# Matmuls of two K-steps interleaved, and weight blocks 160 columns apart in the rotating places

## The reference

```python
m, ... = mixer_even(hn, ...)   # z = h @ w_in (1024 x 2048) ... @ w_out (1024 x 1024)
m, cc  = mixer_odd(hn, ...)    # h @ w_in (1024 x 3072) ... @ w_out (1024 x 1024)
x = x + rmsnorm(m, p['norm_mix_post'][l])
hn = rmsnorm(x, p['norm_ffn_pre'][l])
f = jnp.square(jax.nn.relu(hn @ p['mlp_up'][l])) @ p['mlp_down'][l]
x = x + rmsnorm(f, p['norm_ffn_post'][l])
```

## Time and profile before

| what | value |
|---|---|
| median of 3 runs | 2115.71 us (2115.54 to 2116.01) |
| the profiled execution: its own time | 2116.21 us |
| its span, first to last instruction | 2114.1 us |
| PE busy in the span | 2105.2 us |
| granted TensorE clock, mean | 0.999 |
| DVE, ACT, POOL busy | 1187.2, 718.6, 279.3 us |

### The profile page before, as it was taken

How to read it: one execution, slowest core, us unless ns; L and a number is a source line. 1 busy time by engine, 2 the same in 40 slices (tenths; PEclk the granted TensorE clock), 3 DMA queues, 4 the chain that set the end, 5 groups by cost and what they waited for, 6 DMA issues and landing times.

```text
span 2114.1 us, 33629 instructions
## 1 busy us (share of the span) xinstructions
PE 2105.2 (100%) x13976; PEld 2094.1 (99%) x13976; DVE 1187.2 (56%) x1798; ACT 718.6 (34%) x1225; POOL 279.3 (13%) x307
## 2 busy tenths in 40 slices
PE   9999999999999999999999999999999999999998
PEld 9999999999999999999999999999999999999998
DVE  8766367364755747334953333384566475564336
ACT  6673345132232322333511112352313233232332
POOL 2000000031221312000033232000113022130000
PEclk9999999999999999999999999999999999999999
DMA  4111422111111111141311114131111111111142
GB/s 165 39 38 40 137 78 85 51 51 42 51 48 51 51 51 51 42 141 40 123 51 40 51 50 133 41 122 51 45 52 45 51 51 51 51 51 46 46 142 82
DMA packets 209189, 138.78 MB, mean 66 GB/s; under 512 B 6768, under 2 KB 205552, under 8 KB 209040
## 3 DMA queue, kind: packets, MB, share of 16 engines
q1 hardware_dynamic: 208320, 135.51, 21.1%
q10 hardware_dynamic: 720, 1.13, 0.1%
HBM read 119.22 MB, written 17.40 MB: 65 GB/s over the span
## 4 chain that ended last, share of the span: by engine, by line
PE 89%; issue 10%; DMA 0%; POOL 0%; DVE 0%; DVEq 0%; ACTq 0%; SPq 0%; POOLq 0%
PE ps L881 23%; PE ps L882 23%; PE ps L883 23%; PE ps L927 6%; PE ps L929 6%; PE ps L930 6%; PE ps L1003 1%; PE ps L1031 0%; PE ps L957 0%; PE ps L948 0%; DMA w_all_raw<-in_w_in_even_dram 0%; PE ps L944 0%; DMA w_all_raw<-in_mlp_down_dram 0%; PE ps L1014 0%; PE ps L990 0%
## 5 line engine op out<-in xcount | busy, mean ns | idle before, releaser
L881 PE MATMUL ps<-x_hi,w_all 128*128 128x352 f32 x2304 | 751.4, 326 | 0.0
L883 PE MATMUL ps<-x_hi,w_all 128*128 128x352 f32 x2304 | 739.4, 321 | 0.0
L882 PE MATMUL ps<-x_lo,w_all 128*128 128x352 f32 x2304 | 739.3, 321 | 0.0
L882 PEld LDWEIGHTS ps<-x_lo,w_all 128*128 128x128 f32 x2304 | 433.6, 188 | 2.2
L881 PEld LDWEIGHTS ps<-x_hi,w_all 128*128 128x128 f32 x2304 | 432.6, 188 | 2.7
L883 PEld LDWEIGHTS ps<-x_hi,w_all 128*128 128x128 f32 x2304 | 432.3, 188 | 0.0
L1116 ACT CAST w_all<-w_all_raw 128x1024 fp32r<-128x1024 f32 (+1 forms) x166 | 199.8, 1204 | 422.0 <-DMA w_all_raw<-in_mlp_up_dram 167.6
L927 PE MATMUL ps<-h_hi,w_all 128*128 128x264 f32 x1120 | 318.9, 285 | 0.0
L929 PE MATMUL ps<-h_lo,w_all 128*128 128x264 f32 x1120 | 318.6, 284 | 0.0
L930 PE MATMUL ps<-h_hi,w_all 128*128 128x264 f32 x1120 | 318.0, 284 | 0.0
L1635 DVE SCALAR_TENSOR_TENSOR tmp<-ps,rstd 128x352 f32<-128x352 f32 x192 | 100.1, 522 | 284.6 <-PE ps L883 284.5
(11 more groups left out here) (225 smaller groups left out, 2415.5 us busy)
## 6 DMA issues: line engine op xcount, KB each, us to landing
w_all_raw<-in_mlp_up_dram SPq DMA_DIRECT2D x60, 512.0 KB, 3.9
w_all_raw<-in_mlp_down_dram SPq DMA_DIRECT2D x96, 256.0 KB, 3.1
x_save<-f SPq DMA_DIRECT2D x9, 1408.0 KB, 6.5
x_old<-x_save SPq DMA_DIRECT2D x9, 1408.0 KB, 11.7
w_all_raw<-in_c_w_in_dram SPq DMA_DIRECT2D x22, 512.0 KB, 3.6
w_all_raw<-in_w_in_even_dram SPq DMA_DIRECT2D x12, 512.0 KB, 3.6
w_all_raw<-in_mlp_down_dram SPq DMA_DIRECT2D x12, 512.0 KB, 4.0
x_old<-in_x_cols_dram SPq DMA_DIRECT2D x3, 1408.0 KB, 11.2
```

The lines of the kernel that those rows point to most:

```text
L881: nc.tensor.matmul(dst, wh, hi, start=(i == 0), stop=False)
L882: nc.tensor.matmul(dst, wh, lo, start=False, stop=False)
L883: last = nc.tensor.matmul(dst, wl, hi, start=False, stop=(i == len(order) - 1))
```

## The change

In `unit(n)` the K-steps are taken two at a time. Where the order of matmuls was (high, high-low, low) of step 0, then the same three of step 1, it is now: high weights by high data of steps 0 and 1, high weights by low data of steps 0 and 1, low weights by high data of steps 0 and 1. What `between` inserts after an even K-step now comes after the odd one, and the waits for both steps stand before the six matmuls. `product`, `first_high` and `first_low` keep their order.

In the rotating places the blocks of a load of 352-column units now start 160 columns apart (640 bytes, where it was 512), each still 128 wide; the low parts start 1280 columns into the place. The pair loads of the seven products keep their layout, and so do the places `s`, `x`, `ha` and `hb`. As 2560 columns are now in use, the scratch of the norms moves out of the place into a tensor of its own, `sums`.

```diff
-        sq_sum = [w_all_raw[:, 0, 2 * D + t * TT:2 * D + (t + 1) * TT].rearrange("p (j c) -> p j c", c=QUAD)
-                  for t in range(NT)]
-        fold = [w_all_raw[:, 0, 2 * D + NT * TT + 16 * i:2 * D + NT * TT + 16 * i + NJ] for i in range(8)]
+        sums = place("sums", [P, TOK + 8 * 16], F32)
+        sq_sum = [sums[:, t * TT:(t + 1) * TT].rearrange("p (j c) -> p j c", c=QUAD) for t in range(NT)]
+        fold = [sums[:, TOK + 16 * i:TOK + 16 * i + NJ] for i in range(8)]
...
-                size = FORMS if LOADS[l].pair else D
-                three = [w[:, s, i * size:(i + 1) * size].rearrange("p (k n) -> p k n", n=P)
+                step = P if LOADS[l].pair else P + 32
+                size = FORMS if LOADS[l].pair else KC * step
+                three = [w[:, s, i * size:(i + 1) * size].rearrange("p (k n) -> p k n", n=step)[:, :, 0:P]
...
-                    hi, lo = pt(src[0], k, t), pt(src[1], k, t)
-                    wh, wl = w_k(l, 0, w0 + k), w_k(l, 1, w0 + k)
-                    nc.tensor.matmul(dst, wh, hi, start=(i == 0), stop=False)
-                    nc.tensor.matmul(dst, wh, lo, start=False, stop=False)
-                    last = nc.tensor.matmul(dst, wl, hi, start=False, stop=(i == len(order) - 1))
+                    if i % 2 == 0:
+                        continue
+                    two = order[i - 1:i + 1]
+                    for j in two:
+                        nc.tensor.matmul(dst, w_k(l, 0, w0 + j), pt(src[0], j, t), start=(j == order[0]), stop=False)
+                    for j in two:
+                        nc.tensor.matmul(dst, w_k(l, 0, w0 + j), pt(src[1], j, t), start=False, stop=False)
+                    for j in two:
+                        last = nc.tensor.matmul(dst, w_k(l, 1, w0 + j), pt(src[0], j, t), start=False,
+                                                stop=(j == order[-1]))
                     if i == len(order) - 1:
                         last.then_inc(pe_unit, 1)
+                    between(n, i - 1)
                     between(n, i)
```

## The result

| | before | after |
|---|---|---|
| median | 2115.86 us (2115.54 to 2116.26, 4 runs) | 2132.78 us (2132.01 to 2133.33, 4 runs) |
| ratio | | 1.0080, 95% interval 1.0062 to 1.0097 |
| span of the profiled execution | 2114.1 us | 2130.0 us |

The change costs 17 us. The forecast of 2108 has the wrong sign; the time lies inside the range of 2085 to 2134, and it is rival D that happened.

A forecast was written before the change was run, and what follows sets the result against it. PE, busy throughout, was taken as the bound, set by matmul count times start-to-start distance. From the profiled 2116.2 us, 7.7 came off for the order and 0 for layout and hidden costs: 2108.5, median 2108.0 us, range 2085 to 2134.

The forecast's parts named there:

- rival D: Matmuls of `unit`: never-repeated weights make each load collide with the stream, 26 us more at most, likely 2121 to 2141; chance 0.28.
- What bounds the kernel: PE: busy throughout; matmul count times start-to-start distance sets the end, and only the distance, 158.8 ns in `unit`, can move.
- Part 1: K-steps by twos in `unit`: without repeated weights, 3424 line-881 matmuls lose 2.25 ns each, 7.7 us in all.
- The bad end of this part: All 10,272 matmuls of `unit` slow to the opening units' 161.3 ns from 158.8: 26 us more.
- Part 2: Blocks 160 columns apart in the rotating places: priced at 0, between -38 and +26 us.
- The two rules: Skill page: independent ports would leave 2115.7 us; an isolated 352-column matmul takes 149.2 ns. Lengths in one unit oppose the first.
- Costs hidden by other work: Rounding over gaps, smaller DMA pieces and later inserted matmuls priced at 0, with up to 1 us allowed in the opening.
- the cover of 1.2 us: Phase starts: DVE ends x 1.2 us before PE needs it, covering 0.48 us of delay; uncovered, three phases pay up to 0.5.
- the slack of 0.21 us: Gates inserted by `between`: 0.21 us stays before a gate must wait for ACT to read the previous gate's bank.
- What will show it: Signs in the profile: count stays 13,976, line means tell the rivals apart, 264-column lines 284 to 285, PE waits below 3 us.
- The other sign: Matmul distances: the prediction is wrong if they leave 155 to 162 ns, as all bounds come from the old order.
- B: Matmuls of `unit`: both parts together make most distances short, 20 us or more of 38 gained, 2078 to 2098; chance 0.20.

The follow-up runs named there:

- e10: Kernel before, old order and 128-column blocks, all blocks of the rotating places moved by 32 columns, norm scratch in its own tensor: 2115.11 us, ratio 0.9996.
- e2: Kernel before with only the new layout (blocks 160 columns apart, norm scratch moved), old order of matmuls: 2123.05 us, ratio 1.0034.
- e11: Kernel before, old order, with blocks 160 columns apart and moved by 32 columns (128 bytes): 2129.28 us, ratio 1.0064.
- e3: Changed kernel with the blocks in the rotating places moved by 32 columns (128 bytes), no instruction changed: 2126.77 us, 1.0052 of the kernel before.
- e6: Kernel before with K-steps of a 352-column unit in the order even chunks first, then odd, blocks 160 columns apart: 2125.83 us, ratio 1.0048.
- e1: Kernel before with only the new order by twos, blocks still 128 columns apart: 2132.55 us, ratio 1.0079.
- e9: Changed kernel, order by twos, with blocks 192 columns (768 bytes) apart instead of 160: 2133.16 us, 1.0083 of the kernel before.
- e7: Kernel before, old order, with blocks 192 columns (768 bytes) apart and the norm scratch moved: 2117.97 us, a single time.
- e4: Kernel before with the second and third matmul of each K-step exchanged, so no load repeats the weights before it: 2115.90 us, ratio 0.9999.
- e5: Kernel before with K-steps of a 352-column unit in the order even chunks first, then odd, blocks 128 columns apart: 2118.76 us, ratio 1.0014.

## Why the prediction was wrong

The kernels that the rule speaks of in one table: the share of matmuls whose relation is opposite, worked out from order and layout, and the mean and the median distance in ns over the units of eight K-steps in the rotating places, from 390 us on, without those that have a small matmul inserted or stand right behind one (88 to 98 units in each tile).

| kernel | order, blocks | opposite: tiles 0 and 2 | tile 1 | means, tile 0 / 1 / 2 | medians | us |
|---|---|---|---|---|---|---|
| before | old, 128 | half, by K-step | half | 159.3 / 159.1 / 159.2 | 158.9 / 159.0 / 159.1 | 2115.9 |
| e10 | old, 128, +32 | half, by K-step | half | 159.1 / 159.1 / 159.1 | 158.9 / 159.1 / 159.0 | 2115.1 |
| e2 | old, 160 | two of three | one of three | 159.1 / 161.1 / 159.3 | 158.9 / 161.1 / 159.5 | 2123.1 |
| e11 | old, 160, +32 | one of three | two of three | 161.1 / 159.4 / 161.1 | 161.1 / 159.5 / 161.1 | 2129.3 |
| after | twos, 160 | none | all | 161.5 / 159.7 / 161.5 | 161.1 / 159.3 / 161.2 | 2132.8 |
| e3 | twos, 160, +32 | all | none | 159.5 / 161.5 / 159.7 | 158.9 / 161.2 / 159.3 | 2126.8 |
| e6 | even first, 160 | all but two | two | 159.8 / 160.2 / 160.3 | 158.9 / 160.0 / 158.9 | 2125.8 |
| e1 | twos, 128 | half, each time | half | 161.6 / 159.7 / 161.6 | 161.7 / 158.5 / 161.7 | 2132.6 |
| e9 | twos, 192 | half, each time | half | 161.6 / 159.7 / 161.6 | 161.7 / 158.5 / 161.7 | 2133.2 |

**How far the rule reaches.** It gives the sign where order and block distance stay and the blocks move by 128 bytes (after and e3, e2 and e11), and e10 and e7, which are like before, and e9, which is like e1, agree with it. It does not give the price of the order. Before and e1 both have half of their matmuls opposite, and e1 is 16.7 us slower; in e1 tile 1 is 2 to 3 ns faster than tiles 0 and 2 with the same half. That the order costs 16.7 us is shown; what in it costs them is not. The obvious rival is that the chunk, and with 128-column blocks the relation, now changes at every matmul and not at every third; no run tests it by itself.

**What bounds the kernel, and that only the distance can move.** Right: 14.1 of the 15.9 us are distances between the matmuls of `unit`.

**Part 1, the failed step.** The sum took 7.7 us off because "each line-881 distance loses 323 - 321 = 2 ns" once no load repeats its weights. It loses nothing, since the repeat never cost anything (e4, ratio 0.9999). And the condition in front of it, that the new matmuls "behave like lines 882 and 883", failed too: e1 costs 16.7 us where 7.7 were to be gained. I had two readings of the same row, the repeated weights and the place in the K-step behind a change of chunk, and took the first without a row that separates them. The bad end of this part came near: the opening units, at 161.3 ns, have the number that tiles 0 and 2 took (161.6 in e1). Tile 1 came to 159.7, so a little over half of D's full price of 26 us was paid, 14.1 us in the changed kernel and 15.2 in e1. But the row was read too firmly. 12 of its 40 matmuls have their weights in `w_s` and not in a rotating place, and eight of these took 1.30 us, 162 ns each, in a place that I had called the better one:

```profile
12.78 0.81 PE L944 MATMUL ps<-x_hi,w_s 128*128 128x352 f32 x4
13.43 0.81 PE L948 MATMUL ps<-x_lo,w_s 128*128 128x352 f32 x4
14.08 0.81 PE L957 MATMUL ps<-x_hi,w_all 128*128 128x352 f32 x4
```

And the same kind of stretch takes 157.3 ns in the changed kernel and 162.5 in e2 (last section). That it had D's number here is in part luck.

**Part 2, priced at 0.** Its first half was right: the relation becomes the same in all K-steps of a tile and differs between tiles, as 352 columns are 1408 bytes. It then said that "the layout by itself is a gain in no row", and took 0. The row of `x`, 160.8 in the second tile, was the price: with the layout of `x` the rotating places behave like `x`. One tile of three at 2 ns on the 9216 matmuls of the rotating places is 6.1 us; e2 has 6.2 in its units (1654.62 against 1648.46). In the new order the same layout has tiles 0 and 2 on the bad side, and moved by 128 bytes (e3) only tile 1. So the 0 came out for the layout on top of the new order (16.9 against 16.7 us in e1), but by luck: alternation at each matmul and a fixed bad relation happen to cost about the same in tiles 0 and 2.

**Which load is it?** The table separates two readings. Tile 0 with 160 apart has each matmul's data and its own weights in opposite halves in both orders, yet it is at 159.1 in e2 and 161.5 after. Taken with the weights that are being fetched beside it, the relation is opposite for two of three in the old order (chunk k beside block k twice, then block k + 1) and never in the new one (always the neighbouring block). The sign goes with this second reading in all four kernels with blocks 160 apart. With the load after the next the sign would turn in all four, "opposite" being the bad side; e5 and e6, where nearly every load has the same relation whichever is taken, have opposite as the good side and so leave the second reading. That it is two reads that meet is argued from the table; no run shows it directly.

**The two rules.** After all runs stands what the trace said: e3 and the changed kernel have the same instructions in the same order, and 128 bytes in the start of the blocks move the time by 6.0 us. The rule of the Trainium skill in "TensorE: Matmul & The Clock Gate" ("Step-by-step: what each phase is for"), that the load of the next weights takes nothing from the running matmul, doesn't agree with these runs as the prediction read it; by that reading e3, e2 and e11 would all have stood at 2115.7, and they took 2126.77, 2123.05 and 2129.28.

**Costs hidden by other work.** Rounding and subtracting over gaps took what they took before; from the page and the groups by form:

```profile
L1123 ACT CAST w_all<-w_all_raw 128x1024 fp32r<-128x1024 f32 x126 | 131.7, 1045 | 270.2 <-DMA w_all_raw<-in_mlp_up_dram 169.1 <-DMA w_all_raw<-in_c_w_in_dram 56.1 <-DMA w_all_raw<-in_mlp_down_dram 23.2
...
L1473 DVE TENSOR_TENSOR w_all<-w_all_raw,w_all 128x1024 fp32r<-128x1024 f32 x126 | 153.3, 1216 | 17.9 <-ACT w_all L1123 17.9
```

The loads landed a little later, as the issues of the page show against the earlier trace rows, 4.0 for 3.6 us and 3.7 for 3.6. After the opening no unit waited for one; in the opening PE waited 0.6 us for the rounding of `w_all`, as the list of waits above has it:

```profile
w_all_raw<-in_c_w_in_dram SPq DMA_DIRECT2D x22, 512.0 KB, 3.7
w_all_raw<-in_w_in_even_dram SPq DMA_DIRECT2D x12, 512.0 KB, 4.0
```

In the opening I had allowed up to 1 us: it is 0.5, and 1.1 in e2. Where x of a phase is late, the cover of 1.2 us stood: DVE ends at 341.43 + 4.04 = 345.47, PE starts on it at 346.73, and the list of waits has nothing there.

```profile
341.43 4.04 DVE L1547 SCALAR_TENSOR_TENSOR x_lo<-f,vecs,x_hi 128x352 fp32r<-128x352 f32 x8
...
346.73 0.48 PE L884 MATMUL ps<-x_hi,h_hi 128*128 128x352 f32 x2
```

The gates never made PE wait either, as the slack of 0.21 us said; that in five places another inserted matmul now follows a gate was in no term, and only moves 1.2 us from `unit` to the gates.

**What will show it.** The page carried D's sign: no line fell to 321. But D's 323 to 324 for both loops' lines is met in the stretch only as 322.7, because one tile of three stayed fast. A mean over tiles hides this; the starts of the units don't. As it said, the tiles differ more than before (159.3, 159.1 and 159.2 ns before, 161.5, 159.7 and 161.5 after), the 264-column lines stay at 284 to 285, and PE's waits stay below 3 us (2.2). The other sign, that distances leave the range of 155 to 162 ns, came too: of the matmuls in the units of the table 15.5% are over 162 in the changed kernel and 38% in e1, up to 170. But 6% are over it in the kernel before as well; one unit was too few to take the range from.

**Bounds.** Two of them were off by the prediction's own numbers, which changes nothing in the outcome: B with 20 us less ends at 2096, not 2098, and 2134 leaves out a third of D's 20 us, not a quarter.

## What to carry to other kernels

On a kernel that is bound by back-to-back matmuls, lay a unit's starts side by side tile by tile before touching order or layout, and write down for each matmul where its data and the weights fetched beside it lie within 256 bytes. A change of order alone turns such relations over, and here it had a price that the relations don't explain, so order and start address have to be tried together; here the old order with 128-column blocks was as good as any other of the thirteen kernels. And where one row has two readings, the exchange of two matmuls (e4) tells them apart for the price of one run.

## What the runs showed of the hardware

- Matmuls of 352 fp32r columns at the full granted clock (0.999 in every run) stand 154 to 170 ns apart, one by one, in the units of the table, with nothing waiting. Within one order the median per unit depends on addresses modulo 256 bytes: 158.9 to 159.5 on the good side and 161.1 to 161.2 on the bad one with the old order and with the twos, 158.9 and 160.0 with even chunks first.
- A load that repeats the weights before it costs and saves nothing (e4, 0.9999).
- The distance depends on what ran before, too. The opening units have the same order and the same blocks, 160 apart, in e2 and in the changed kernel. The fours of the changed kernel:

```profile
12.22 0.79 PE L955 MATMUL ps<-x_lo,w_all 128*128 128x352 f32 x4
...
18.51 0.79 PE L964 MATMUL ps<-x_hi,w_all 128*128 128x352 f32 x4
```

and those of e2:

```profile
12.42 0.81 PE L949 MATMUL ps<-x_lo,w_all 128*128 128x352 f32 x4
...
19.57 0.65 PE L945 MATMUL ps<-x_hi,w_all 128*128 128x352 f32 x3
```

40 matmuls in 6.29 us are 157.3 ns each; 44 in 7.15 us are 162.5. Both then stay so through the opening. In e1 and e9 too, units of tile 1 with equal addresses come at 158.5 or at 161.5, and units in the place `x` at anything from 156.6 to 163.6; in the changed kernel 11 of 92 units of tile 1 stand at 163.5 and the others at 159 to 159.5; in e6 it is 162 and 158.9. So something besides the addresses decides, and it can last for many matmuls. That it is a state carried from matmul to matmul is a guess. What it is stays open, as does why all and two of three opposite come to the same mean.
